# A two-layer decoder trunk on one NeuronCore: the widest-stride outputs are scaled by DVE as it evacuates them, and the order of work changes in the opening and at the end of the last set

## The reference, cut to what matters

```python
DIL_GROUPS = ((128, 1), (512, 4), (2048, 16))      # window, dilation
for g, (window, dil) in enumerate(DIL_GROUPS):
    q = _partial_rope(_rmsnorm(proj[:, :, g, 0], q_gain[g]), positions)
    k = _partial_rope(_rmsnorm(proj[:, :, g, 1], k_gain[g]), positions)
    o, lse = _dilated_group(q, k, proj[:, :, g, 2], window, dil)
    outs.append(o); lses.append(lse)
wts = jax.nn.softmax(jnp.stack(lses, axis=0), axis=0)
o = jnp.einsum('gbsh,gbshe->bshe', wts, jnp.stack(outs, axis=0))
x = x + o.reshape(B, S, H * Dh) @ w_out
x = x + jnp.square(jax.nn.relu(rmsnorm(x) @ w1)) @ w2
```

## Time and profile before

| what | value |
|---|---|
| median of 3 runs | 1539.22 us (1538.27 to 1540.44) |
| the profiled execution's own time | 1538.35 us |
| its span (first to last instruction) | 1536.3 us |
| PE busy | 1520.2 us, 99% of the span |
| PEclk | 9 or more in all 40 slices (granted clock 1.00) |
| DVE / ACT / POOL busy | 61% / 46% / 25% |
| DMA | 173.57 MB, mean 113 GB/s |

### The profile page before, as it was taken

The page is one execution under the profiler, slowest core; times in us unless marked ns, Lnnn a source line. Parts: engine busy times, 40 slices in busy tenths (PEclk is TensorE's granted clock), DMA queues, the critical chain, the costliest instruction groups (busy, mean ns, idle before and its releaser), DMA issues.

```text
span 1536.3 us, 24840 instructions
## 1 busy us (share of the span) xinstructions
PE 1520.2 (99%) x9312; PEld 1232.1 (80%) x9312; DVE 937.3 (61%) x1659; ACT 702.3 (46%) x1191; POOL 386.1 (25%) x515
## 2 busy tenths in 40 slices
PE   8999999999999999999999999999998999999998
PEld 7777777888888888888878877887877888888887
DVE  5457644557484769646546576656545475665678
ACT  6334354453544545544434344444353453535353
POOL 3301100220110511343338253425622210101010
PEclk9999999999999999999999999999999999999999
DMA  6221110567565754432222422222314566665753
GB/s 180 71 75 50 62 37 30 164 141 199 117 182 129 184 140 83 151 110 70 83 73 81 127 66 71 70 82 81 101 57 150 152 122 194 122 191 118 206 113 83
DMA packets 111600, 173.57 MB, mean 113 GB/s; under 512 B 12688, under 2 KB 45456, under 8 KB 111504
## 3 DMA queue, kind: packets, MB, share of 16 engines
q1 hardware_dynamic: 91904, 134.51, 28.1%
q0 software_dynamic: 17408, 33.56, 13.4%
q10 hardware_dynamic: 2192, 4.20, 0.8%
HBM read 165.89 MB, written 6.36 MB: 112 GB/s over the span
## 4 chain that ended last, share of the span: by engine, by line
PE 90%; POOL 4%; DVE 2%; ACT 1%; SPq 1%; issue 1%; DMA 1%; POOLq 0%; ACTq 0%; DVEq 0%
PE ps L657 57%; PE ps L976 20%; PE ps L791 3%; PE ps L736 3%; PE ps L764 2%; PE ps L803 2%; POOL qrs L1898 1%; PE ps L704 1%; PE ps L728 1%; DVE qn L1442 0%; ACT p_sb L1133 0%; DMA w_raw<-in_dil_w_out 0%; POOL o_ring L1927 0%; POOL rt L1907 0%; POOL qn L1910 0%
## 5 line engine op out<-in xcount | busy, mean ns | idle before, releaser
L657 PE MATMUL ps<-w_h,act_h 128*128 128x512 f32 x768 | 309.0, 402 | 2.0 <-DVE act_l L1402 1.1
L657 PE MATMUL ps<-w_l,act_h 128*128 128x512 f32 x768 | 301.7, 393 | 0.0
L657 PE MATMUL ps<-w_h,act_l 128*128 128x512 f32 x768 | 301.6, 393 | 0.0
L1380 DVE SCALAR_TENSOR_TENSOR w_l<-w_raw,gain_t,w_h 128x512 fp32r<-128x512 f32 x186 | 141.4, 802 | 98.1 <-ACT w_h L1056 97.9
L657 PE MATMUL ps<-act_h,w_h 128*128 128x512 f32 x512 | 199.6, 390 | 0.0
L657 PE MATMUL ps<-act_l,w_h 128*128 128x512 f32 x512 | 199.2, 389 | 0.0
L657 PE MATMUL ps<-act_h,w_l 128*128 128x512 f32 x512 | 199.2, 389 | 0.0
L1898 POOL TENSOR_TENSOR qrs<-qss,m_half 128x8 f32<-128x8 f32 x64 | 110.5, 1726 | 309.4 <-DVE qss L1426 304.6
L657 PEld LDWEIGHTS ps<-w_h,act_h 128*128 128x128 f32 x768 | 152.1, 198 | 32.1 <-issue 3.1
L657 PEld LDWEIGHTS ps<-w_l,act_h 128*128 128x128 f32 x768 | 152.1, 198 | 28.6
L976 PE MATMUL ps<-w_h,op_h 128*128 128x512 f32 x448 | 174.4, 389 | 0.0
(11 more groups left out here) (228 smaller groups left out, 2429.2 us busy)
## 6 DMA issues: line engine op xcount, KB each, us to landing
w_raw<-in_dil_w_in SPq DMA_DIRECT2D x72, 512.0 KB, 3.7
raw<-in_mlp_w SPq DMA_DIRECT2D x64, 512.0 KB, 4.7
raw<-in_mlp_w POOLq DMA_DIRECT2D x48, 512.0 KB, 5.8
w_raw<-in_mlp_w SPq DMA_DIRECT2D x32, 512.0 KB, 4.9
w_raw<-in_fox_w_in SPq DMA_DIRECT2D x22, 512.0 KB, 3.7
p_sb<-in_mlp_w SPq DMA_DIRECT2D x16, 512.0 KB, 4.8
pT_sb<-in_mlp_w SPq DMA_DIRECT2D x16, 512.0 KB, 5.4
w_raw<-in_mlp_w POOLq DMA_DIRECT2D x16, 512.0 KB, 6.7
```

Of the source, the lines that this page charges most:

```text
L657: return mm(ps_out, lhs[i], rhs[j], start=(k == 0 and term == 0), stop=(k == KT - 1 and term == 2))
L1380: last = v.scalar_tensor_tensor(w_l[u % WR][:, j, :], raw(u)[:, j, :], gain_t[:, norm, k:k + 1], f(w_h[u % WR][:, j, :]), ALU.mult, ALU.su ...
```

## The change

- **Widest stride.** For kind 2, `output` on DVE waits for the head's factors and writes `o_ring` = PSUM x factor 1 in one tensor_tensor. POOL's `merge` no longer has that multiplication for kind 2. For all kinds POOL multiplies the accumulator before it waits for the output.
- **Opening.** ACT and DVE do their part of turned x tiles ahead of the bank's other work. `gw_l` moves to the start of DVE's bank 2. In the turns of the second lone projection (set 2) the fourth moves from (5, 5) to (5, 6).
- **Last set.** DVE normalises at even ticks, behind maxima and outputs, one tick later than before; the last head pair is normalised inside `out_projection`. Two turned pieces move from ticks 8 and 12 to 9 and 13. On ACT both `probs_back` of a pair stand ahead of both `factors`.
- **Output projection of the second layer.** x tiles 0, 1 and 3 are fetched back by ACT at tick 17 of the last step, tile 2 after the last merge. On DVE `split_low` of units 4 and 5 stands ahead of the last normalising and of the eighth turned piece.

```diff
-TURNS_ALONE = {0: [(2, 6), (3, 5), (4, 4), (5, 4)], 2: [(3, 1), (3, 7), (4, 5), (5, 5)]}
+TURNS_ALONE = {0: [(2, 6), (3, 5), (4, 4), (5, 4)], 2: [(3, 1), (3, 7), (4, 5), (5, 6)]}
...
-TURN_TICKS = {1: [2, 4, 6, 8, 10, 16, 22], 7: [2, 3, 4, 6, 8, 12, 18]}
+TURN_TICKS = {1: [2, 4, 6, 8, 10, 16, 22], 7: [2, 3, 4, 6, 9, 13, 18]}
...
 (ACT step)
                             if probs_back_on_act(attend):
                                 probs_back(attend, TICK0[attend] + h - 2)
+                    for h in heads:
+                        if 2 <= h <= len(ticks_of(attend)) + 1:
                             factors(attend, TICK0[attend] + h - 2)
...
+                        if attend == len(SETS) - 1 and a == n - 3:
+                            act.wait_ge(acc_out, 32)
+                            act.wait_ge(merged, 3 * HS)
+                            act.wait_ge(x_out, 16 * NT)
+                            for t in (0, 1, 3):
+                                x_again(t)
                     for s, b in banks_of_tick(proj, attend, a):
-                        bank_event(s, b, attend)
                         if s == 0 and b < 2:
                             prepare(0, 0, b + 2)
                             prepare(0, 1, b + 2)
+                        bank_event(s, b, attend)
...
+            def x_again(t):
+
+                act.dma_start(x_sb[:, t, :], x_dram[t * P:(t + 1) * P, :]).then_inc(x_back[t], 16)
...
 (ACT out_projection)
                     act.wait_ge(merged, 4 * HS)
-                    act.wait_ge(x_out, 16 * NT)
-                    for t in range(NT):
-                        act.dma_start(x_sb[:, t, :], x_dram[t * P:(t + 1) * P, :]).then_inc(x_back[t], 16)
+                    x_again(2)
...
 (DVE bank_event, now at its head; removed behind the sums and from forget_gates)
+                if s == 0 and b < 2:
+                    prepare(0, 0, b + 2)
+                    prepare(0, 1, b + 2)
+                if s == 0 and b == 2:
+                    dve.wait_ge(gwh_done, 2)
+                    v.tensor_tensor(gw_l[:, :, :], gw_raw[:, :, :], f(gw_h[:, :, :]), ALU.subtract).then_inc(gwl_done, 1)
...
 (DVE output)
+                    if kind == 2:
+                        dve.wait_ge(efac_done, m + 1)
+                        v.tensor_tensor(o_ring[:, m % 2, :, 0:VC], o_ps[:, :, 0:VC],
+                                        e_fac[:, m % 4, 1, :].unsqueeze(2).broadcast_to([P, NT, VC]), ALU.mult).then_inc(o_done, 1)
+                        return
...
 (DVE step)
-                        if SETS[attend][0] == 0 and a % 2 == 1 and a >= 5:
+                        if SETS[attend][0] == 0 and paired(attend) and a % 2 == 0 and a >= 6:
+                            for h in (a - 6, a - 5):
+                                if tl[h][2]:
+                                    normalise(attend, tl[h][0])
+                        if SETS[attend][0] == 0 and not paired(attend) and a % 2 == 1 and a >= 5:
                             for h in (a - 5, a - 4):
...
             def out_projection(B0, prep):
+                split_low(B0 + 4)
+                if prep == 4:
+                    split_low(B0 + 5)
+                    for h, _, last_bank in ticks_of(len(SETS) - 1)[-2:]:
+                        normalise(len(SETS) - 1, h)
                 prepare(prep, 1, 3)
-                split_low(B0 + 4)
-                split_low(B0 + 5)
+                if prep == 1:
+                    split_low(B0 + 5)
...
 (POOL merge)
-                pool.wait_ge(o_done, a + 1)
-                g.tensor_tensor(acc, acc, e_fac[:, m % 4, 0, :].unsqueeze(2).broadcast_to([P, NT, VC]), ALU.mult)
-                link(g.tensor_tensor(new, new, e_fac[:, m % 4, 1, :].unsqueeze(2).broadcast_to([P, NT, VC]), ALU.mult))
+                earlier = g.tensor_tensor(acc, acc, e_fac[:, m % 4, 0, :].unsqueeze(2).broadcast_to([P, NT, VC]), ALU.mult)
+                if kind == 2:
+                    link(earlier)
+                    pool.wait_ge(o_done, a + 1)
+                else:
+                    pool.wait_ge(o_done, a + 1)
+                    link(g.tensor_tensor(new, new, e_fac[:, m % 4, 1, :].unsqueeze(2).broadcast_to([P, NT, VC]), ALU.mult))
                 g.tensor_tensor(acc, acc, new, ALU.add).then_inc(merged, 1)
```

More of the change, by code:

```diff
@@ L1427, in bank_event @@
                                     ALU.add).then_inc(qss_done, 1)
-                if s == 0 and b < 2:
-                    prepare(0, 0, b + 2)
-                    prepare(0, 1, b + 2)
                 if attend is None and b < QK_SET:
@@ L1604, in forget_gates @@
                                     ALU.mult).then_inc(gwh_done, 1)
-                if b == 2:
-                    dve.wait_ge(gwh_done, 2)
-                    v.tensor_tensor(gw_l[:, :, :], gw_raw[:, :, :], f(gw_h[:, :, :]), ALU.subtract).then_inc(gwl_done, 1)
                 if b == 4:
```

## The result

| what | before | after |
|---|---|---|
| median of the runs of this comparison | 1539.83 us (1538.27 to 1541.51, 4 runs) | 1528.01 us (1527.72 to 1528.32, 4 runs) |
| ratio, 95% interval | | 0.9923 [0.9906, 0.994] |
| the profiled execution's own time, its span | 1538.35, 1536.3 us | 1528.32, 1526.3 us |

The change takes 11.8 us off the medians and 10.0 us off the profiled executions. The forecast was a gain of 9.35. By the ratio, 0.9923 x 1539.22 = 1527.4 us, just beyond the fast end of the range (1528.0).

A forecast was written before the change was run, and what follows sets the result against it. PE was taken as the bound, busy 1520.2 of 1536.3 us, so only its waits could be won. Terms 1.83 + 0.45 + 1.64 + 2.33 - 0.70 + 3.80 = 9.35 gave 1529.0, plus 0.87, 1529.9 us; 8-in-10 range 1528.0 to 1533.9.

The forecast's parts named there:

- the runs' median lies 0.87 above it, so 1529.9: Last step of the sum: 0.87 us added to the 1529.0 forecast from the profiled execution, giving the runs' median.
- Opening and set 2: Waits for `act_l` and `gw_l` in the opening, 1.83 us saved; set 2's fourth turning, 0.45 saved.
- Widest stride: Two PE waits for POOL in set 7's projection shortened by moving the product to DVE: 1.64 us saved, lower end 0.99.
- Ticks: Last set: DVE's normalising no longer ahead of maxima and output copy; 2.33 us saved, less 0.70 at two turnings.
- The two new waits: Turnings at ticks 9 and 13: each waits 0.15 to 0.5 us anew, 0.35 taken, together -0.7.
- The eighth turning: PE's eighth turned piece, its normalising now behind two splits: cost taken as 0, at most 0.7 us.
- Output projection: Second layer's tail: second pair of weights ready at least 5.6 us earlier, removing waits of 3.80 us.
- The tail stayed late: Rival: second pair of weights still lands after PE wants it, giving back 3.80: 1533.7 us. Chance 0.10.
- The eighth and the moved turnings became a wait: Rival: eighth turning costs 0.7, ticks 9 and 13 cost 1.0, opening gives back 1.1: 1532.0 us. Chance 0.14.
- The product did help POOL: Rival claimed the opposite: DVE's multiplication holds POOL's reads and the two turnings wait as before: 1531.5 us. Chance 0.08.
- never by `e_fac`: Slower rival: DVE waits for `e_fac` at each of 16 widest-stride outputs; at 0.9 us a head, 1544.3 us. Chance 0.03.
- The waits did not merely move: Rival claimed saved time is lost in the same chain's next wait, or PE's rate changes: about 1537 us. Chance 0.07.

The follow-up runs named there:

- e10: Kernel before with 8 and 12 added identity transposes, results overwritten, ahead of the third and fourth turning of x in the tail: 1540.9 us, ratio 1.0009.
- e12: Kernel before with 4 and 6 added identity transposes, results overwritten, ahead of the third and fourth turning of x in the tail: 1538.48 us, ratio 0.9995.
- e3: Kernel before with only even-tick normalising, two moved turned pieces, ACT's pair order and the last pair normalised first in `out_projection`: 1537.45 us, ratio 0.9989.
- e4: Kernel before with only the early splits of units 4 and 5 and three x tiles fetched back early: 1534.5 us, ratio 0.9969.
- e5: Changed kernel with all four x tiles fetched after the last merge, splits still early: 1530.13 us.
- e6: Changed kernel with both splits behind the last normalising and the eighth turned piece, x tiles still fetched early: 1529.46 us.
- e8: Changed kernel with the two moved turned pieces at ticks 10 and 14 instead of 9 and 13: 1527.38 us, ratio 0.9923.
- e9: Changed kernel with turned pieces at ticks 10 and 14 and the second unit's split behind the last normalising and eighth piece: 1526.76 us, ratio 0.9919.
- e7: Changed kernel, but DVE first copies the widest-stride output into `o_ring` and multiplies it there, both inputs in SBUF: 1528.44 us, ratio 0.993.

## Why the prediction came out as it did

**The failed step** is "the runs' median lies 0.87 above it, so 1529.9". The 0.87 was carried over as a constant of the measurement. The runs show in its place a loss that the change removes: two thirds of the runs of the kernel before have a mean clock under 1.000 and lie 1.6 us higher, the profiled one was not among them, and in kernels without the tail's waits the profiled execution and the median agree within 0.3 us (1528.32 and 1528.01). With nothing carried over the forecast would have been 1529.0. That PE's stalls in the tail bring the lowered clock is shown by e10 and e12, which fill them: 20 of their 22 runs have 1.000, against 18 of 56. That the loss in the typical run sits where e3 shows it, and costs that much, rests on that one trace, on e12's median and on e4's six even runs; no trace of a run of the kernel before with a lowered clock was taken.

The forecast of 1529.9 is 1.9 us above the measured 1528.01, and 2.5 above the 1527.4 by the ratio. The constant is 0.87 of this (and 0.3 more, since the profiled run after lies above its median), the sum the other 0.7: 10.0 between the profiles against 9.35. The forecast's own range, gains of 7.9 to 10.9, doesn't follow from the ends that it states: with those (1.1 given back in the opening, 0.99 for the widest stride, -1.0 and -0.7 at the turnings, or nothing lost there) the sum runs from 6.6 to 10.05. The profiles' 10.0 lies at the upper end of that and the medians' 11.8 beyond both.

- *Opening and set 2*: 2.08 and 0.52 against 1.83 and 0.45. Right, with the 0.16 added to each wait; nothing was given back by the pushed split.
- *Widest stride*: 2.08 against 1.64, the most mis-sized term. The two turnings gave 0.28 and 1.34 (priced 0.37 and 1.27), and the power of the last bank came 1.3 us nearer to its sum, two merges' worth as taken, though not up to it. The other 0.46 came at three matmuls of the projection between 1051 and 1094 us, short stops that the modelled ends hide and that the list of waits doesn't have; the term put them at nothing. Alone the part gave 2.4 in its trace, because POOL's earlier merges also shortened the normalising's waits, which the forecast had given wholly to the ticks. DVE's product cost nothing: 424 ns against the copy's 422.
- *Ticks*: 1.42 against 1.63. The two new waits are 0.36 each (0.20 + 0.16), the 0.35 taken. The eighth turning waited 0.41 for its normalising, taken as 0, bound 0.7.
- *Output projection*: 4.01 against 3.80. Right. ACT had the second pair of weights at 1163.38 instead of 1178.33, 9.0 us sooner beyond PE's own lead of 6.0, where 5.6 was taken as the least; x tile 2's late landing held its add 1.06 us, hidden.

**The rivals.** The tail stayed late in e5 and e6, not in the change. The eighth and the moved turnings became a wait of 0.36 + 0.36 + 0.41 = 1.1 us together, against 0.7 in the sum, and e8 and e9 got it back. The product did help POOL. The Trainium skill (Perfetto Trace Analysis, Optimizing Scalar/DVE Operations) had warned that such a move might not. The traces agree with the Trainium skill (SBUF — State Buffer, Who interferes with whom), as L1571, L1392 and e7's L1572 above show. The rival could have been weighed from before: there DVE's mask, a tensor_tensor out of PSUM and SBUF, stands beside POOL's operation, which keeps its usual 0.62 us.

```profile
887.07 0.70 DVE L1478 TENSOR_TENSOR ps<-ps,banded 128x512 f32<-128x512 f32 x1 [1.40 <-PE ps L736]
887.38 0.62 POOL L1926 TENSOR_TENSOR o_sb<-o_sb,e_fac 128x260 f32<-128x260 f32 x1
```

DVE's new product is held up by PE alone (7.8 us of idle time, all ended by L781), never by `e_fac`. The waits did not merely move.

## What to carry to other kernels

When the runs' median lies above a profiled execution with a clean clock, list the runs by granted clock before treating the gap as a constant: a change that removes PE's stalls can win it as well. Price a stage's waits as a chain, not one by one, since a shorter chain on a helper engine pays again in the next stage, and the next stage that is bound on its own takes it back. Where DVE has to touch the data in PSUM anyway, try moving GpSimd's work on it there: the product was free in this kernel.

## What the runs showed of the hardware

- PE's granted clock fell to the lower level for 3.4 us behind stalls of 0.98 and 1.60 us in a program where PE is 99% busy, at a cost of 1.7 us (e3's profiled run). Runs with a mean clock of 1.000 and runs below it occur with the same kernel (18 and 38 of 56).
- POOL's 128x260 operations take 0.62 to 0.70 us beside a DVE instruction from PSUM, mostly 0.95 to 1.18 beside splits of 128x512 out of SBUF. In the changed kernel the one sum that met two splits of 128x1024 took 1.68, and the splits 2.87 us instead of 2.35.
- A DVE product of 128x260 with both inputs in SBUF took 0.43 us, and 0.88 where a POOL operation of that size had started 0.03 us before it (e7).
